# SSD scan: where a group's squares, rounded gates and remainders stand in the queues of ScalarE and VectorE

## The chip, the cores and the metric

The kernel runs on one core of a Trainium2 chip. The metric is the device time of one execution in microseconds (us): 1591.27 before the change, the median of three runs (1589.19 to 1595.38). A core has five engines, each of which works off its own queue of instructions in the written order: TensorE (PE in the profile; PEld is its weight load), VectorE (DVE), ScalarE (ACT), GpSimd (POOL) and SyncE (SP, which issues the transfers). They wait for each other through semaphores only, written out by hand.

## The reference, cut to what matters

One step of a two-layer trunk on 384 tokens (128 of context, 256 latent) with 1024 channels, in float32. The first layer's mixer is a Mamba-2 scan (SSD) in both directions with 32 heads in 8 groups, chunks of 128 tokens:

```python
acum = jnp.cumsum(dtc * a_neg.reshape(ng, nr), axis=2)
decay = jnp.exp(jnp.where(mask, acum[:, :, :, None] - acum[:, :, None, :], -jnp.inf))
scores = jnp.einsum('bcign,bcjgn->bcijg', cc, bc)
y_intra = jnp.einsum('bcijgr,bcjgrp->bcigrp', scores[..., None] * decay, xdt)
states = jnp.einsum('bcqgn,bcqgr,bcqgrp->bcgrpn', bc, decay_end, xdt)
y_inter = jnp.einsum('bcign,bcgrpn,bcigr->bcigrp', cc, s_prev, jnp.exp(acum))
...
y = y_f + flip_seq(y_b) + xs * d_skip[:, None]
y = rms_norm(y.reshape(bsz, seqlen, SSD_D_INNER) * jax.nn.silu(z), norm_w)
return y @ w_out, s_f, s_b
```

The gated rows y * silu(z) go through an RMS norm (so the sum of their squares is needed) and then into the output projection. In the kernel a float32 product with weights is made of three passes over rounded parts: an operand is split into a rounded value ("hi") and its remainder ("lo", the value minus the rounded one).

## The kernel before, in words

The scan takes the groups g = 0 to 7 one after the other, and in each the three chunks u = 3g, 3g+1, 3g+2 (context, first and second latent chunk). All tiles stay in SBUF. Five functions, `ssd_pe`, `ssd_act`, `ssd_dve`, `ssd_pool` and `ssd_sp`, write out the queue of each engine by hand; nothing is planned or reordered. Work for the next group begins before a group is done: the token rows, masked scores and segment sums of chunks 3g+3 to 3g+5 stand in group g's part of the queues.

TensorE, per chunk: `turn_rows` transposes the chunk and forms its scores, `segment(u)` sums the decay exponents of both directions from rounded rows (`decay_rows`, GpSimd) and their remainders (`rows_lo`, ScalarE, L1322), `outputs(u)` (L1500) multiplies the decayed scores. Per group: `states` (L1462), `entry_decays` (L1475) and `entry` (L1487) for the states that enter the two latent chunks. Between these it multiplies blocks of the conditioning weights for the other sub-layers (`conditioning`, L402): 14 blocks in group 0, then 10 a group in groups 1 to 3 and 9 in groups 4 to 7. `conditioning(g, 0, 2)`, right behind `states(g)`, waits until VectorE has added the bias to the block before, `conditioned(g-1)` (L413).

ScalarE: `token_rows` (L1285) copies the transposed rows, `decays` (L1289) takes the exponent of a segment, `entry_decays` (L1301) that of the entry decays. `gates_out(g)` makes, for the two tiles of a finished group, two squares (L1307 or L1311) and two rounded gates `yhi` (L1313).

VectorE: `masked` (L1572) masks the scores, `decayed` (L1580) multiplies them by the decays, `new_state` (L1591) carries the states, `entered` (L1598 to L1601) weights the entering states' rows, `gated_out` (L1609 to L1617) adds them, the skip and the gate. `gates_lo(g)` makes the two remainders `ylo` of a finished group (L1622); it waits for `yhi`.

GpSimd makes `xdt`, `xw`, `sdec` and the rounded decay rows, and at the end of a group's part sums the squares (`square_sums`, L1406). Behind the last group it splits the first two blocks of the output weights (`split_one_lo`, L332).

Behind the scan, VectorE finishes the modulation vectors of all sub-layers in small steps (L1667 to L1672). `back_act` waits for the last of them before ScalarE's third split of output weights (L320), and the output projection (`back_pe`, L819 to L821) takes its tiles of gates in order: tiles 0 to 7 in its first block, 8 to 15 in its second.

Of the kernel before, what the change touches and what calls it, by code (L numbers as in the profile page):

```python
# [122 lines left out]
def trunk(nc, io):  # L123
    ctx = ExitStack()
    with ctx:
# [72 lines left out]
        def v(name):  # L198
            a, b = VEC[name]
            return vec[:, a:b]  # L200
# [121 lines left out]
        def split_first(act, name):  # L322

            for k in range(2):
                split_hi(act, phase[name], Idx(k))
# [198 lines left out]
        def ada_rows(act, bank, n):  # L524
            act.activation(arow[:, :], ps[:, bank, 0:P], ACT.Copy).then_inc(ada_row, 1)
# [719 lines left out]
        def h4(ap):  # L1245
            return ap.rearrange("p (h n) -> p h n", h=4)
# [6 lines left out]
        def ssd_begin(eng):  # L1253
            eng.wait_ge(dt_tok, 2)
            eng.wait_ge(tok_split, 2)
            eng.wait_ge(dt_dec, 1)
            eng.wait_ge(conv_silu, 2 + CONV_T)
            eng.wait_ge(blk_done, phase["ssd_in"].own0 + N_IN + SPL)
# [17 lines left out]
        def ssd_act(act):  # L1276
            ssd_begin(act)

            def token_rows(u):
                g, c = u // 3, u % 3  # L1280
                act.wait_ge(s_a, u + 1)
                if g >= 2:
                    act.wait_ge(s_xdt, u - 5)
                    act.wait_ge(s_st, 2 * g - 2)
                act.activation(xtok[:, g % 2, c, :], ps[:, 0, 0:TOK], ACT.Copy).then_inc(s_xtok, 1)  # L1285

            def decays(u):
                act.wait_ge(s_seg, u + 1)
                act.activation(ps[:, 1 + u % 2, :], ps[:, 1 + u % 2, :], ACT.Exp).then_inc(s_exp, 1)  # L1289

            def state_out(g):
                act.wait_ge(s_st, 2 * g + 1)
                if g:
                    act.wait_ge(s_out[(g - 1) % 2], 16 * ((g - 1) // 2 + 1))
                act.activation(st_sb[:, :], ps[:, 4, :], ACT.Copy).then_inc(s_stout, 1)

            def entry_decays(g, k):
                act.wait_ge(s_eb, 2 * g + k + 1)
                if g:
                    act.wait_ge(s_bw, 2 * g - 1 + k)  # L1300
                act.activation(e_in[:, k].rearrange("p d n -> p (d n)"), ps[:, 4 + k, :], ACT.Exp).then_inc(s_ee, 1)  # L1301

            def gates_out(g):
                act.wait_ge(s_v, 3 * g + 3)
                for t in (2 * g, 2 * g + 1):
                    if g == 0:
                        act.activation(rms_sum[t % 2][:, :], gate[:, t, :], ACT.Square).then_inc(rms_sq, 1)  # L1307
                    else:
                        if g > 1:
                            act.wait_ge(rms_add, t - 3)  # L1310
                        act.activation(rms_new[t % 2][:, :], gate[:, t, :], ACT.Square).then_inc(rms_sq, 1)  # L1311
                for t in (2 * g, 2 * g + 1):
                    act.activation(yhi[:, t, :], gate[:, t, :], ACT.Copy, scale=nw[:, t:t + 1]).then_inc(y_hi, 1)  # L1313

            def rows_lo(u):
                g, c = u // 3, u % 3
                if u:
                    act.wait_ge(s_seg, u)
                for d in range(2):
                    for h in range(4):  # L1320
                        n = 4 * g + 32 * d + h
                        i = act.activation(seg_lo[:, d, h * P:(h + 1) * P], masks[:, 1 + d, :], ACT.Copy,  # L1322
                                           scale=tok_lo[:, c, n:n + 1].bitcast(F32))
                i.then_inc(s_rlo, 1)

            nw = v("ssd_norm")
            rows_lo(0)
            for c in range(NCH):
                token_rows(c)
            decays(0)  # L1330
            rows_lo(1)
            for g in range(SSD_G):
                more = g + 1 < SSD_G
                decays(3 * g + 1)
                state_out(g)
                rows_lo(3 * g + 2)
                act.wait_ge(s_stout, g + 1)
                act.dma_start(io["o_ssd"][g], st_sb[:, :].rearrange("p (d n) -> p d n", d=2)).then_inc(s_out[g % 2], 16)
                entry_decays(g, 0)
                if more:  # L1340
                    token_rows(3 * g + 3)
                decays(3 * g + 2)
                if g:
                    gates_out(g - 1)
                entry_decays(g, 1)
                if more:
                    rows_lo(3 * g + 3)
                    token_rows(3 * g + 4)
                    decays(3 * g + 3)
                    rows_lo(3 * g + 4)  # L1350
                    token_rows(3 * g + 5)
                act.wait_ge(ada_used, ADA_1 + ADA_G[g + 1])
                act.wait_ge(ada_tr, g + DT)
                ada_rows(act, 3, ADA_G[g + 1] - ADA_G[g])
            split_first(act, "ssd_out")
            gates_out(SSD_G - 1)
# [205 lines left out]
        def ssd_dve(dve):  # L1562
# [12 lines left out]
            def decayed(u):  # L1575
                dve.wait_ge(s_exp, u + 1)
                dve.wait_ge(s_gm, u + 1)
                if u >= 2:
                    dve.wait_ge(s_y, u - 1)
                dve.tensor_tensor(ge_s[:, u % 2].rearrange("p d (h n) -> p d h n", h=4),  # L1580
                                  h4(ps[:, 1 + u % 2, :]).unsqueeze(1).to_broadcast([P, 2, 4, P]),
                                  gm_s[:, u % GM].unsqueeze(2).to_broadcast([P, 2, 4, P]), ALU.mult).then_inc(s_ge, 1)

            def new_state(g):
                b = g % 2
                dve.wait_ge(s_st, 2 * g + 2)
                if g >= 2:
                    dve.wait_ge(s_in, 2 * g - 2)
                for d in range(2):
                    dve.wait_ge(s_dec, 2 * g + d + 1)  # L1590
                    dve.tensor_tensor(s1[:, b, d, :], sdec[:, d, :], ps[:, 5, d * 256:(d + 1) * 256],  # L1591
                                      ALU.add).then_inc(s_new, 1)

            def entered(g, k):
                n = 2 * g + k
                f, w = ps[:, 4 + k, 0:256], ps[:, 4 + k, 256:512]
                dve.wait_ge(s_in, n + 1)
                dve.tensor_tensor(w, w, e_in[:, k, 1, :], ALU.mult).then_inc(s_fw, 1)  # L1598
                dve.tensor_tensor(y_in[:, k, :], f, e_in[:, k, 0, :], ALU.mult).then_inc(s_fw, 1)
                dve.wait_ge(s_fw, 2 * n + 2)  # L1600
                dve.tensor_tensor(y_in[:, k, :], y_in[:, k, :], w, ALU.add).then_inc(s_bw, 1)  # L1601
# [17 lines left out]
            def gates_lo(g):  # L1619
                for t in (2 * g, 2 * g + 1):  # L1620
                    dve.wait_ge(y_hi, t + 1)
                    dve.scalar_tensor_tensor(ylo[:, y_lo_tile(t), :], gate[:, t, :], nw[:, t:t + 1],  # L1622
                                             yhi[:, t, :].bitcast(F32), ALU.mult, ALU.subtract).then_inc(y_lo, 1)

            def conditioned(g):
                dve.wait_ge(ada_tr, g + DT + 1)
                ada_bias(dve, 3, ADA_1 + ADA_G[g], ADA_G[g + 1] - ADA_G[g]).then_inc(ada_ready, 1)
# [5 lines left out]
            for g in range(SSD_G):  # L1633
                u = 3 * g
                decayed(u + 1)
                if g:
                    conditioned(g - 1)
                new_state(g)
                gated_out(u)
                masked(u + 3)  # L1640
                decayed(u + 2)
                if g:
                    gates_lo(g - 1)
                entered(g, 0)
                masked(u + 4)
                gated_out(u + 1)
                if g + 1 < SSD_G:
                    decayed(u + 3)
                entered(g, 1)
                masked(u + 5)  # L1650
                gated_out(u + 2)
# [10 lines left out]
            for m in range(1, 2 * DEPTH):  # L1662
                lay, part = m // 2, 3 * (m % 2)
                g, b = (v(x).rearrange("p (n t) -> p n t", n=4)[:, m - 1, :].unsqueeze(2).to_broadcast([P, DT, 2])
                        for x in ("ln_g", "ln_b"))
# [9 lines left out]
        def y_lo_tile(t):  # L1675

            return t // 2 + 8 * (t % 2)
# [1541 lines left out]
```

## Time and profile before

| | |
|---|---|
| median of three runs | 1591.27 us (1589.19 to 1595.38) |
| profiled execution | 1593.25 us, span of its trace 1591.3 us |
| busy: TensorE, VectorE, ScalarE, GpSimd | 97%, 55%, 50%, 57% of the span |
| granted TensorE clock, mean | 0.983 of full speed |
| the SSD scan | from about 238 to 404 us |
| one of the groups 1 to 6 | 19.0 to 19.8 us |

The shares are means over the whole program. Only the stretch of the scan, 10% of the span, holds the instructions that the change moves, so the rows below are cut from it. A busy time is that of an engine's own instructions; the bracket behind a row gives the idle time just before it and what ended it.

### The profile page before, as it was taken

The page shows a single profiled execution, that of the slowest core. Times are in us where ns is not written, and L with a number is a line of the kernel's source. Part 1 is how long each engine was busy: PE and PEld are TensorE (multiplying, and loading weights), DVE is VectorE, ACT ScalarE, POOL GpSimd, SP SyncE. Part 2 cuts the span into 40 slices and gives each one's busy share as a digit, 9 for nine tenths or more (in the row PEclk, how much of TensorE's full clock was granted, in tenths as well). Part 3 has the DMA queues.
Part 4 walks back from the last instruction along what each step waited for, and adds up shares of the span by engine and source line. Part 5 has one row for each costly group of instructions (what it writes and reads, how often), then busy time and mean ns, then how long its engine had stood idle before and what let it go on. Part 6 is the DMA issues. An engine that isn't in the chain of part 4 may idle for free.

```text
span 1591.3 us, 31239 instructions
## 1 busy us (share of the span) xinstructions
PE 1536.7 (97%) x11879; PEld 1460.3 (92%) x11879; DVE 871.2 (55%) x1814; ACT 799.3 (50%) x1461; POOL 905.8 (57%) x516
## 2 busy tenths in 40 slices
PE   8999998999999999999999999999989999999996
PEld 6999996877999999999999989888789999999996
DVE  3453104777437777712673448598883357777323
ACT  3655436776336444423776554555554345544323
POOL 2555556677572555557245556787764725555552
PEclk9999999999999999999999999999989999999998
DMA  9333437877451343434124323101123523434431
GB/s 378 121 120 119 127 125 251 307 285 277 148 165 55 119 132 122 156 112 153 53 93 161 107 89 110 42 28 49 38 87 114 154 80 106 132 120 141 133 122 40
DMA packets 58020, 209.67 MB, mean 132 GB/s; under 512 B 6321, under 2 KB 6449, under 8 KB 57649
## 3 DMA queue, kind: packets, MB, share of 16 engines
q1 hardware_dynamic: 56752, 205.96, 39.3%
q10 hardware_dynamic: 1152, 2.10, 0.4%
q8 instruction: 81, 1.33, 0.3%
q14 instruction: 35, 0.28, 0.1%
HBM read 200.63 MB, written 7.41 MB: 131 GB/s over the span
## 4 chain that ended last, share of the span: by engine, by line
PE 70%; issue 9%; DVE 8%; POOL 7%; ACT 3%; DMA 2%; POOLq 0%; DVEq 0%; SPq 0%; ACTq 0%
PE ps L911 6%; PE ps L913 6%; PE ps L912 6%; PE ps L819 6%; PE ps L821 6%; PE ps L820 6%; POOL wlo L332 4%; PE ps L2905 3%; PE ps L2907 3%; PE ps L2906 3%; PE ps L1155 3%; PE ps L1157 3%; PE ps L1156 3%; PE ps L402 2%; DVE ps L2478 1%
## 5 line engine op out<-in xcount | busy, mean ns | idle before, releaser
L332 POOL TENSOR_TENSOR wlo<-raw,whi 128x1024 fp32r<-128x1024 f32 (+1 forms) x191 | 484.2, 2536 | 412.1 <-ACT whi L320 411.7
L320 ACT ACTIVATE whi<-raw 128x1024 fp32r<-128x1024 f32 (+1 forms) x237 | 261.4, 1103 | 500.0 <-PE ps L821 185.4
L911 PE MATMUL ps<-hhi,whi 128*128 128x384 f32 x656 | 219.8, 335 | 2.5 <-POOL wlo L332 2.0
L985 DVE SCALAR_TENSOR_TENSOR evac<-ps,vec,evac 128x189 f32<-128x189 f32 (+3 forms) x440 | 166.5, 412 | 97.1 <-ACT evac L926 67.5
L913 PE MATMUL ps<-hhi,wlo 128*128 128x384 f32 x656 | 219.2, 334 | 0.0
L912 PE MATMUL ps<-hlo,whi 128*128 128x384 f32 x656 | 219.1, 334 | 0.0
L2670 POOL TENSOR_TENSOR wlo<-raw,whi 128x1024 fp32r<-128x1024 f32 x46 | 111.2, 2418 | 124.2 <-ACT whi L320 124.2
L2905 PE MATMUL ps<-hhi,whi 128*128 128x384 f32 x368 | 126.9, 345 | 0.7 <-POOL wlo L2670 0.7
L911 PEld LDWEIGHTS ps<-hhi,whi 128*128 128x128 f32 x656 | 123.1, 188 | 4.4 <-issue 3.2
L2907 PE MATMUL ps<-hhi,wlo 128*128 128x384 f32 x368 | 123.9, 337 | 0.0
L2906 PE MATMUL ps<-hlo,whi 128*128 128x384 f32 x368 | 123.8, 337 | 0.0
L879 DVE SCALAR_TENSOR_TENSOR xr<-ps,ada,xr 128x128 f32<-128x128 f32 x64 | 23.8, 413 | 182.0 <-PE ps L821 181.8
L912 PEld LDWEIGHTS ps<-hlo,whi 128*128 128x128 f32 x656 | 123.2, 188 | 0.0
L913 PEld LDWEIGHTS ps<-hhi,wlo 128*128 128x128 f32 x656 | 123.1, 188 | 0.0
L1155 PE MATMUL ps<-hhi,whi 128*128 128x384 f32 x360 | 120.5, 335 | 0.6 <-POOL wlo L332 0.6
L1157 PE MATMUL ps<-hhi,wlo 128*128 128x384 f32 x360 | 120.3, 334 | 0.0
L1156 PE MATMUL ps<-hlo,whi 128*128 128x384 f32 x360 | 120.3, 334 | 0.0
L819 PE MATMUL ps<-ghi,whi 128*128 128x384 f32 x352 | 118.6, 337 | 1.3 <-POOL wlo L332 1.3
L821 PE MATMUL ps<-ghi,wlo 128*128 128x384 f32 x352 | 117.6, 334 | 0.0
L820 PE MATMUL ps<-glo,whi 128*128 128x384 f32 x352 | 117.6, 334 | 0.0
L819 PE MATMUL ps<-yhi,whi 128*128 128x384 f32 x256 | 87.1, 340 | 2.3 <-POOL wlo L332 2.3
L820 PE MATMUL ps<-ylo,whi 128*128 128x384 f32 x256 | 85.6, 334 | 0.0
(379 smaller groups left out, 3587.7 us busy)
## 6 DMA issues: line engine op xcount, KB each, us to landing
raw<-w_in_in SPq DMA_DIRECT2D x98, 512.0 KB, 3.5
raw<-w_up_in SPq DMA_DIRECT2D x88, 512.0 KB, 3.5
raw<-w_ada_in SPq DMA_DIRECT2D x80, 512.0 KB, 4.5
raw<-w_down_in SPq DMA_DIRECT2D x32, 704.0 KB, 4.1
raw<-w_out_in SPq DMA_DIRECT2D x32, 512.0 KB, 3.8
first_ada<-w_ada_in SPq DMA_DIRECT2D x16, 512.0 KB, 10.0
qe<-e_keep SPq DMA_DIRECT2D x8, 512.0 KB, 6.8
s<-s_ssd_in SPq DMA_DIRECT2D x8, 256.0 KB, 4.2
```

What stands on the lines that cost most here:

```text
L320: act.activation(whi[:, z.mod(SPL), 0:p.kt * P], raw[:, b.mod(RAW), 0:p.kt * P], ACT.Copy).then_inc(hi_ready, 1)
L332: pool.tensor_tensor(wlo[:, z.mod(SPL), 0:p.kt * P], raw[:, b.mod(RAW), 0:p.kt * P], whi[:, z.mod(SPL), 0:p.kt * P].bitcast(F32), ALU.subt ...
L819: pe.matmul(out, a, rhi[:, h, :], start=(r == 0), stop=False)
L820: pe.matmul(out, a, rlo[:, l, :], start=False, stop=False)
L821: mm = pe.matmul(out, b, rhi[:, h, :], start=False, stop=(r == 2 * p.kt - 1))
L911: pe.matmul(out, a, hhi[:, k, :], start=(k == 0), stop=False)
L912: pe.matmul(out, a, hlo[:, k, :], start=False, stop=False)
L913: mm = pe.matmul(out, b, hhi[:, k, :], start=False, stop=(k == DT - 1))
L1155: pe.matmul(out, a, hhi[:, k, :], start=(k == 0), stop=False)
L2905: pe.matmul(out, a, hhi[:, k, :], start=(k == 0), stop=False)
L2906: pe.matmul(out, a, hlo[:, k, :], start=False, stop=False)
L2907: mm = pe.matmul(out, b, hhi[:, k, :], start=False, stop=(k == DT - 1))
```

## The change

ScalarE: `gates_out(g - 1)` stood between `decays(3 * g + 2)` and `entry_decays(g, 1)`. It now stands behind `token_rows(3 * g + 4)` and ahead of `decays(3 * g + 3)`; what was between comes sooner. VectorE: `gates_lo(g - 1)` stood between `decayed(u + 2)` and `entered(g, 0)`. It now stands between `decayed(u + 3)` and `entered(g, 1)`. In the last group, where there is no `decayed(u + 3)`, it follows `gated_out(u + 1)`. No instruction is added, removed or altered, and no wait is.

```diff
                     token_rows(3 * g + 3)
                 decays(3 * g + 2)
+                entry_decays(g, 1)
+                if more:
+                    rows_lo(3 * g + 3)
+                    token_rows(3 * g + 4)
                 if g:
                     gates_out(g - 1)
-                entry_decays(g, 1)
-                if more:
-                    rows_lo(3 * g + 3)
-                    token_rows(3 * g + 4)
+                if more:
                     decays(3 * g + 3)
                     rows_lo(3 * g + 4)
                     token_rows(3 * g + 5)
...
                 masked(u + 3)
                 decayed(u + 2)
-                if g:
-                    gates_lo(g - 1)
                 entered(g, 0)
                 masked(u + 4)
                 gated_out(u + 1)
                 if g + 1 < SSD_G:
                     decayed(u + 3)
+                if g:
+                    gates_lo(g - 1)
                 entered(g, 1)
                 masked(u + 5)
                 gated_out(u + 2)
```

## Rows read from the trace of the kernel before

**Rows 1.** The page's first part: busy us, share of span, instructions.
```profile
PE 1536.7 (97%) x11879; PEld 1460.3 (92%) x11879; DVE 871.2 (55%) x1814; ACT 799.3 (50%) x1461; POOL 905.8 (57%) x516
```

**Rows 2.** Busy time of one scan group: PE, PEld, DVE, ACT, POOL; clock, DMA.
```profile
329.50:348.50 19.00, 18.87 (x280) 15.47 (x279) 14.22 (x29) 13.76 (x39) 14.55 (x15) 1.00 0.84 302
```

**Rows 3.** List of waits, 240 to 405: us in total, times, longest.
```profile
PEld ps L402 <- DVE ada L413: 4.1, 7, 0.8
```

**Rows 4.** Timeline of VectorE at a group's end: start, us, instruction, idle before.
```profile
324.60 1.22 DVE L1580 TENSOR_TENSOR ge_s<-ps,gm_s 128x1024 f32<-128x1024 f32 x1 [0.19 <-ACT ps L1289]
...
327.32 0.42 DVE L1572 TENSOR_TENSOR gm_s<-ps,masks 128x256 f32<-128x256 f32 x1 [0.38 <-ACT xtok L1285]
...
329.20 1.23 DVE L1580 TENSOR_TENSOR ge_s<-ps,gm_s 128x1024 f32<-128x1024 f32 x1
330.34 0.17 DVE L413 TENSOR_TENSOR ada<-ps,vec 128x20 f32<-128x20 f32 x1
```

**Rows 5.** Timeline of TensorE, conditioning blocks that waited.
```profile
321.16 0.65 PE L402 MATMUL ps<-raw,scond 128*32 128x128 f32 x16 [0.52 <-DMA raw<-w_ada_in]
...
330.56 0.81 PEld L402 LDWEIGHTS ps<-raw,scond 128*32 128x32 f32 x32 [0.47 <-DVE ada L413]
```

**Rows 6.** Timeline of all engines, group 3: entry decays, squares, rounded gates, next decays.
```profile
316.32 1.09 PE L1475 MATMUL ps<-masks,small 128*64 128x128 f32 x16
...
316.92 0.93 ACT L1311 ACTIVATE rms_new<-proj 128x384 f32<-128x384 f32 x2
...
317.75 1.11 ACT L1313 ACTIVATE yhi<-proj,vec 128x384 fp32r<-128x384 f32 x2
...
323.99 0.58 ACT L1289 ACTIVATE ps<-ps 128x512 f32<-128x512 f32 x1 [1.94 <-PE ps L1452]
```

**Rows 7.** Remainders and GpSimd: line L1622 (ns min/median/max), then timelines of groups 1 and 3.
```profile
L1622 DVE SCALAR_TENSOR_TENSOR ylo<-proj,vec,yhi x16: 618/967/1961, 280.2 to 407.1; 128x384 fp32r<-128x384 f32 x16
...
280.18 1.50 POOL L1377 TENSOR_TENSOR xw<-xtok,small 128x256 f32<-128x256 f32 x2
280.24 1.85 DVE L1622 SCALAR_TENSOR_TENSOR ylo<-proj,vec,yhi 128x384 fp32r<-128x384 f32 x2
...
317.92 1.90 POOL L1366 TENSOR_TENSOR seg_hi<-masks,tok_hi 128x1024 fp32r<-128x1024 f32 x1
318.39 2.73 DVE L1622 SCALAR_TENSOR_TENSOR ylo<-proj,vec,yhi 128x384 fp32r<-128x384 f32 x2
...
327.37 0.61 POOL L1377 TENSOR_TENSOR xw<-xtok,small 128x256 f32<-128x256 f32 x1 [4.63 <-ACT xtok L1285]
```

**Rows 8.** Timeline of all engines at the end of group 5.
```profile
362.03 0.58 ACT L1289 ACTIVATE ps<-ps 128x512 f32<-128x512 f32 x1 [1.22 <-PE ps L1452]
...
362.81 1.22 DVE L1580 TENSOR_TENSOR ge_s<-ps,gm_s 128x1024 f32<-128x1024 f32 x1
...
365.37 0.42 DVE L1572 TENSOR_TENSOR gm_s<-ps,masks 128x256 f32<-128x256 f32 x1 [0.23 <-ACT xtok L1285]
```

**Rows 9.** Timeline of the scan's end and the output projection's start.
```profile
401.06 4.72 POOL L332 TENSOR_TENSOR wlo<-raw,whi 128x1024 fp32r<-128x1024 f32 x2 [3.88 <-ACT whi L320]
...
401.87 0.43 DVE L1598 TENSOR_TENSOR ps<-ps,e_in 128x256 f32<-128x256 f32 x1
...
411.30 2.00 ACT L320 ACTIVATE whi<-raw 128x1024 fp32r<-128x1024 f32 x2 [4.60 <-DVE vec L1672]
...
414.84 0.45 PE L819 MATMUL ps<-yhi,whi 128*128 128x384 f32 x1 [0.22 <-POOL wlo L332]
```

**Rows 10.** Busy time and granted clock (behind POOL's) around two TensorE gaps.
```profile
250.00:252.00 2.00, 0.91 (x3) 0.77 (x4) 0.00 (x0) 0.95 (x4) 1.14 (x2) 0.92 1.01 414
252.00:254.00 2.00, 2.00 (x6) 1.61 (x5) 0.72 (x1) 0.58 (x1) 1.28 (x1) 0.50 0.82 336
...
1016.00:1018.90 2.90, 0.78 (x70) 0.67 (x63) 2.85 (x5) 2.81 (x7) 2.90 (x4) 1.00 0.13 48
1018.90:1022.00 3.10, 3.10 (x63) 2.43 (x63) 3.07 (x4) 1.72 (x4) 3.10 (x4) 0.63 0.03 8
```

More of the change, by code:

```diff
@@ L1342, in ssd_act @@
                 decays(3 * g + 2)
-                if g:
-                    gates_out(g - 1)
                 entry_decays(g, 1)
@@ L1348, in ssd_act @@
                     token_rows(3 * g + 4)
+                if g:
+                    gates_out(g - 1)
+                if more:
                     decays(3 * g + 3)
@@ L1641, in ssd_dve @@
                 decayed(u + 2)
-                if g:
-                    gates_lo(g - 1)
                 entered(g, 0)
@@ L1648, in ssd_dve @@
                     decayed(u + 3)
+                if g:
+                    gates_lo(g - 1)
                 entered(g, 1)
```

## The prediction

> **What bounds the kernel now.** I read the page first: TensorE is busy for 97% of the span [rows 1], so a change off TensorE counts only where TensorE waits for it. Then the busy time by stretch: one scan group (19 us) has TensorE busy 18.87 us, VectorE 14.22, ScalarE 13.76, GpSimd 14.55 [rows 2]. No other engine is full, and TensorE has hardly any idle time to give back: the reader is to see that the change can gain little and can lose much. The list of waits then says which wait is left: the first conditioning block of a group (L402) waits for VectorE's bias add L413, 7 times, 4.1 us on the weight side [rows 3]. About 0.2 us of each is a gap that other blocks have as well. That wait ends VectorE's chain at the end of a group, which is next in the timeline: `decayed(u+3)` at 324.60, `entered(g,1)`, `masked(u+5)` at 327.32 after 0.38 us idle (for ScalarE's token rows), `gated_out(u+2)`, `decayed(u+4)` at 329.20, L413 at 330.34 [rows 4]; TensorE starts L402 at 330.56 [rows 5]. So from `decayed(u+3)` on, VectorE already sets the end of every group, with 0.38 us of slack.
>
> **ScalarE's part.** Nothing is added; two squares and two rounded gates move from behind `decays(3g+2)` to behind `token_rows(3g+4)`. They take 316.92 to 318.86, 1.94 us [rows 6]. In their new place they stand ahead of `decays(3g+3)`, where ScalarE waits 1.94 us for TensorE's segment today (start 323.99) [rows 6]. What moves ahead is not quite free: `entry_decays(g,1)` must now wait for L1475, which starts at 316.32 and runs 1.09 us, so it begins at 317.41 instead of the squares at 316.92: 0.49 us lost. The queue is through at 323.99 - 1.94 + 0.49 = 322.54, 1.4 us ahead of the segment. I cost ScalarE's move at nothing; the idle 1.94 us is its cover, and if it were gone the score decays, and with them the chain on VectorE, would be late by the excess, at most 1.94 us a group. The segment on TensorE needs `rows_lo(3g+3)`, which comes sooner; no TensorE wait in today's list was for it after group 0, so nothing is gained. GpSimd's sums of squares stand behind `state_decay`, around 328, after the new place of the squares: nothing.
>
> **VectorE's part.** The two remainders (L1622) leave the place ahead of `entered(g,0)` and go between `decayed(u+3)` and `entered(g,1)`: into the chain that ends in L413. Behind them stand `entered`, `masked`, `gated_out`, `decayed(u+4)`, L413, and TensorE's whole queue waits for that. What their old place gives back is idle time: `decayed(u+3)` waits for ScalarE's exponent, not for them, except that in groups 4 to 6 VectorE is a little late. In group 5 the exponent ends at 362.03 + 0.58 = 362.61 and `decayed` starts at 362.81 [rows 8]: 0.16 us comes back beside the usual 0.04.
>
> What do two remainders cost in the new place? Today a pair takes 1.85 us in groups 1 and 2, 2.73 in group 3 [rows 7], because GpSimd is at work. The rows show how: two GpSimd products of 0.61 us each take 1.50 instead of 1.22 while the pair runs, and the pair ends at 280.24 + 1.85 = 282.09, 0.41 us after the GpSimd pair at 281.68. A product of 1.90 us at 317.92 stretches the pair to 2.73. The two engines take turns: each remainder waits out a whole GpSimd instruction, then runs some 0.4 us. In the new place, 325.7 to 326.7, GpSimd is idle: it waits 4.63 us for the token rows and starts at 327.37 [rows 7]. Bounds for the pair are 2 x 0.41 = 0.82 and 1.85; the shortest one alone took 0.618 from start to end [rows 7], and VectorE's instructions overlap by about 0.1. I take 0.95, near the lower end, for GpSimd's idle stretch covers it. The chain absorbs 0.38 us of it in groups 1 to 3 and 0.23 + 0.16 = 0.39 in group 5 (groups 4 and 6 alike). So 0.95 - 0.39 = 0.56 us for each of the six boundaries (groups 1 to 6; group 0 has no remainders, and behind group 7 no conditioning follows): 6 x 0.56 = 3.4 us. It is lost on TensorE in full, as L402 waits already.
>
> **The last group.** There `decayed(u+3)` is absent, so group 6's remainders come directly behind `gated_out(22)`, at 401.87, where `entered(7,1)` starts today [rows 9]. At that time GpSimd splits the first two output weights: 4.72 us for two from 401.06, 2.36 each, the first to 403.42. By the turns of [rows 7] remainder one runs 403.42 to 403.89, split two 403.89 to 406.25, remainder two to about 406.65. `entered(7,1)` starts 4.7 us late, and with it the last gated output, group 7's gates, and the small modulation steps of VectorE; ScalarE's third output split (411.30, waiting for the last of these) and TensorE's third output block (414.84, already waiting 0.22 us for that split) come 4.7 us later [rows 9]. Split two is late by 0.5 us, still ahead of TensorE's second block. No remainder runs beside a weight split in the trace, so both ends stand: without exclusion the shift is the pair alone, 0.95 us; with it 4.7. I take 4.7, since every pair of rows shows turns.
>
> The Trainium skill, page "SBUF — State Buffer", section "Who interferes with whom", says that a VectorE instruction with two SBUF inputs and a GpSimd instruction that reads SBUF cannot run together, and that the one issued second blocks fully. By it the last group costs the 4.7 us above; had remainders and splits run together, 0.95. Rows 7 agree for GpSimd's products; for the weight split no row decides.
>
> **Given back and added.** TensorE's wait for a weight transfer in group 3, 0.52 us [rows 5], goes when the group starts later with its transfers under way: -0.5 (0 to -1). And the clock: where TensorE idled, the granted clock fell to 0.50 of full speed, the 1.2 GHz level: in 250 to 252 it was busy 0.91 us of 2.00, and in 252 to 254 the clock was 0.50; near 1017 it was busy 0.78 of 2.90, then 0.63 over 3.10 us [rows 10]. Lost time: 0.08 x 2 + 0.50 x 2 = 1.16 and 0.37 x 3.1 = 1.15 us. In the last group TensorE now stands still for some 1.6 us ahead of its second block's last tiles (they need group 7's remainders) and about 3.1 ahead of the third block, longer than these gaps: +1.2, between 0 and 2.4. The 0.5 us stalls of the boundaries are too short to compare with them: 0.
>
> Sum: 3.4 + 4.7 - 0.5 + 1.2 = 8.8 us. The profiled execution took 1593.25 us (span 1591.3 and 1.95 around it), so 1602.1 for such a one; it lay 1.98 us above the median 1591.27, hence **1600.1 us**. A measurement tells 0.5% (8.0 us) from no change; the forecast is just past that.
>
> **The rivals.** (a) The turns are not as strict for weight splits, and the tail costs 0.95 with no clock loss: 3.4 + 0.95 - 0.5 = 3.9, 1595.1 us. For: no row shows this pair of operations. Against: three GpSimd forms took turns with L1622. (b) The pair costs in its new place what it costs today, 1.85 us, because GpSimd's products come earlier than I reckon, or ScalarE's four operations do not fit: 6 x (1.85 - 0.39) = 8.8, with 4.7 - 0.5 + 1.2: 14.2, 1605.5 us. Against it: GpSimd's 4.63 us idle. (c) The other side: the remainders hide altogether and TensorE's wait for L413 goes, since entered and masked rows of the group's first half come over a microsecond sooner. That gains the 4.1 us less 7 x 0.2, so -2.7: 1588.6 us. It decides where a pair costs under 0.39 us, the chain's slack; the shortest single remainder is 0.618. (d) As forecast, but the clock holds: 1598.9 us.
>
> **How the numbers follow.** Forecast with clock loss 0.42, (d) 0.15, (a) 0.20, (b) 0.13, (c) 0.06, and 0.04 for what I have not seen. With some 2 us of scatter (the runs shown spread from 1589.19 to 1595.38), slower by over 0.5%, above 1599.2: 0.27 + 0.07 + 0.13 + 0.02 = 0.49. Faster by over 0.5%: no case reaches it by itself; 0.05 with the unseen. The rest, 0.46, within 0.5%. The range reaches to (a) and most of the way to (b): 1594.5 to 1604.5.
>
> **What would show it.** Right: the remainders at the end of a group take about 0.95 us a pair; L413 and TensorE's L402 start about 0.8 us apart from TensorE's last state product instead of 0.3; groups 1 to 6 are 0.5 us longer; ScalarE still waits for the segment ahead of its decays; in the last group remainder one ends with the first weight split, remainder two with the second, and TensorE idles about 3 us ahead of its third output block, with a clock below 1.00 behind it. Wrong: groups of unchanged length, or remainders running inside a weight split. A loop loss of over 1 us a group would say that the pair or ScalarE's queue was mis-sized.

## The result and the profile after

The changed kernel takes 1602.37 us, median of five runs (1600.26 to 1603.74), against 1591.2 us (1589.19 to 1595.38, five runs): ratio 1.006 with a 95% interval of 1.0044 to 1.0075, that is 7.0 to 11.9 us slower. The profiled execution took 1601.72 us, its span 1599.8.

The first part of the page. TensorE's busy time is 1.3 us below that of [rows 1], so on balance the 8.5 us of longer span are idle time; what a slower clock adds at one place has to be offset at another (below):

```profile
PE 1535.4 (96%) x11879; PEld 1460.2 (91%) x11879; DVE 867.0 (54%) x1814; ACT 800.6 (50%) x1461; POOL 902.3 (56%) x516
```

The list of waits between 240 and 440 us (us in total, times, longest). The wait for the bias has grown from 4.1 to 7.3 us on the weight side [rows 3], and the output projection now waits 1.4 us for remainders and 2.9 us for a weight split:

```profile
PEld ps L402 <- DVE ada L413: 7.3, 7, 1.4
PE ps L402 <- DVE ada L413: 4.4, 6, 1.0
PE ps L819 <- POOL wlo L332: 3.6, 2, 2.9
PE ps L819 <- DVE ylo L1623: 1.4, 1, 1.4
```

The timeline at the end of group 3 (lines of VectorE have moved by one; compare [rows 4 to 6]):

```profile
322.48 1.11 ACT L1313 ACTIVATE yhi<-proj,vec 128x384 fp32r<-128x384 f32 x2
...
324.26 0.58 ACT L1289 ACTIVATE ps<-ps 128x512 f32<-128x512 f32 x1 [0.67 <-PE ps L1453]
...
324.88 1.23 DVE L1581 TENSOR_TENSOR ge_s<-ps,gm_s 128x1024 f32<-128x1024 f32 x1 [0.20 <-ACT ps L1289]
...
326.02 1.14 DVE L1623 SCALAR_TENSOR_TENSOR ylo<-proj,vec,yhi 128x384 fp32r<-128x384 f32 x2
...
327.07 0.43 DVE L1599 TENSOR_TENSOR ps<-ps,e_in 128x256 f32<-128x256 f32 x1
...
327.64 0.62 POOL L1378 TENSOR_TENSOR xw<-xtok,small 128x256 f32<-128x256 f32 x1 [5.20 <-ACT xtok L1285]
...
328.20 0.42 DVE L1573 TENSOR_TENSOR gm_s<-ps,masks 128x256 f32<-128x256 f32 x1
...
331.11 0.17 DVE L413 TENSOR_TENSOR ada<-ps,vec 128x20 f32<-128x20 f32 x1
...
331.33 1.08 PE L402 MATMUL ps<-raw,scond 128*32 128x128 f32 x32 [0.55 <-DVE ada L413]
```

The reader is to see the chain of [rows 4] with the remainders in it: they occupy VectorE from 326.02 to 327.07, 1.05 us, while GpSimd stands idle (it starts at 327.64 after 5.20 us); the idle 0.38 us ahead of L1573 has gone; and from `decayed(u+3)` to the bias it is 331.11 - 324.88 = 6.23 us instead of 330.34 - 324.60 = 5.74. (1.05 less 0.38 would be 0.67 us; the other 0.18 were smaller gaps between the chain's instructions, which went as well.) ScalarE still waits 0.67 us for the segment ahead of its decays, so its moved work fits. From one L402 to the next, groups 4 and 5 take 19.56 us each (18.97 and 18.98 before). From group 1's first L402 (271.92) to group 7's (390.43) it is 118.51 us, against 115.00 (272.62 to 387.62): 3.5 us.

The end of the scan, as [rows 9]:

```profile
403.80 5.04 POOL L332 TENSOR_TENSOR wlo<-raw,whi 128x1024 fp32r<-128x1024 f32 x2 [3.21 <-ACT whi L320]
...
404.61 4.64 DVE L1623 SCALAR_TENSOR_TENSOR ylo<-proj,vec,yhi 128x384 fp32r<-128x384 f32 x2
...
415.17 0.41 PE L819 MATMUL ps<-yhi,whi 128*128 128x384 f32 x1 [1.41 <-DVE ylo L1623]
...
418.41 2.00 ACT L320 ACTIVATE whi<-raw 128x1024 fp32r<-128x1024 f32 x2 [4.41 <-DVE vec L1673]
...
421.94 0.69 PE L819 MATMUL ps<-yhi,whi 128*128 128x384 f32 x1 [2.95 <-POOL wlo L332]
```

The pair of remainders starts 0.8 us after the first weight split and ends at 409.25, 0.41 us behind the second one (408.84). From group 7's first L402 to the third output block it is 31.51 us instead of 27.22: 4.3 us. The stretches around that gap (length, busy PE, PEld, DVE, ACT, POOL, then the granted clock), to be read beside [rows 10]:

```profile
419.00:421.94 2.94, 0.00 (x1) 0.01 (x1) 0.16 (x1) 2.91 (x4) 2.40 (x2) 0.78 0.00 0
421.94:424.00 2.06, 2.06 (x6) 2.06 (x7) 1.59 (x4) 0.34 (x1) 2.06 (x1) 0.50 0.33 103
424.00:426.00 2.00, 2.00 (x8) 2.00 (x8) 0.17 (x1) 0.00 (x0) 0.23 (x1) 0.50 0.69 207
426.00:428.00 2.00, 2.00 (x9) 2.00 (x8) 0.00 (x0) 0.00 (x0) 0.00 (x0) 0.62 0.52 211
```

The third block runs at 0.50, the 1.2 GHz level, for most of its length. From its start to the start of the fifth block's split on GpSimd TensorE does the same 33 products without a pause, first before, then after:

```profile
414.84:420.53 5.69, 5.69 (x33) 5.69 (x34) 1.81 (x5) 1.47 (x3) 2.30 (x2) 1.00 0.65 184
```

```profile
421.94:430.17 8.23, 8.23 (x33) 8.23 (x34) 1.76 (x4) 1.47 (x3) 2.29 (x2) 0.66 0.38 127
```

That is 8.23 us instead of 5.69: the clock costs 2.5 us.

So 3.5 + 4.3 + 2.5 = 10.3 us are lost in these two places. The medians differ by 11.2 us, the two profiled spans by 8.5 only, and the rest of the span accounts for the difference. The changed execution reached group 1 0.7 us earlier (271.92 against 272.62). In the second layer, which the change does not touch, TensorE's clock dipped in the execution of before and not in the same stretch of after; from the product at 829.34 (L2936; 838.96 in after) to the one at 840.66 (L2913; 847.15) it is 11.32 us before and 8.19 after, 3.1 less. First before, then after:

```profile
782.00:840.00 58.00, 56.33 (x320) 54.87 (x319) 37.97 (x76) 42.12 (x68) 24.61 (x11) 0.94 0.27 82
```

```profile
791.60:849.60 58.00, 56.34 (x338) 55.15 (x337) 38.52 (x78) 44.33 (x72) 25.70 (x12) 1.00 0.27 82
```

Further on it is the other way round. Both executions wait there for ScalarE, 1.87 us each, but only in after is the clock at half a little later, which costs 1.6 us (from these products to the L1890 ones, 17.14 us before and 18.71 after). Another 0.5 us comes in smaller pieces up to the end. Before, a wait and the stretch behind it, then the same after:

```profile
948.90 0.66 PE L1885 MATMUL ps<-masks,ge 128*128 128x128 f32 x4 [1.87 <-ACT ge L2127]
```

```profile
949.00:952.40 3.40, 3.40 (x22) 3.40 (x23) 3.11 (x4) 2.57 (x3) 2.58 (x2) 1.00 0.31 124
```

```profile
955.39 0.66 PE L1886 MATMUL ps<-masks,ge 128*128 128x128 f32 x4 [1.87 <-ACT ge L2128]
```

```profile
956.60:960.00 3.40, 3.40 (x12) 3.40 (x12) 3.36 (x6) 1.48 (x2) 2.14 (x1) 0.50 0.06 19
```

In all: -0.7 + 10.3 - 3.1 + 1.6 + 0.5 = 8.6, which is the 8.5 up to rounding.

### The profile page after: what moved, and what is told of

Its sections match the earlier page's. It is cut to its first block, busy times and chain, and to the rows that moved or that the text cites. A ratio compares the mean times of both kernels' runs of the same rounds, so it can differ in the third digit from the quotient of the medians.

```text
span 1599.8 us, 31239 instructions
## 1 busy us (share of the span) xinstructions
PE 1535.4 (96%) x11879; PEld 1460.2 (91%) x11879; DVE 867.0 (54%) x1814; ACT 800.6 (50%) x1461; POOL 902.3 (56%) x516
## 4 chain that ended last, share of the span: by engine, by line
PE 69%; DVE 10%; issue 9%; POOL 7%; ACT 3%; DMA 2%; SPq 0%; POOLq 0%; DVEq 0%; ACTq 0%
PE ps L911 6%; PE ps L913 6%; PE ps L912 6%; PE ps L819 6%; PE ps L820 6%; PE ps L821 6%; POOL wlo L332 4%; PE ps L2906 3%; PE ps L2908 3%; PE ps L2907 3%; PE ps L1155 3%; PE ps L1156 3%; PE ps L1157 3%; PE ps L402 2%; DVE ps L2479 1%
```

## The experiments

Each ratio is that of a run to runs of the kernel before on the same chip; the rows come from one profiled execution of each kernel.

**Loop only.** The last group's remainders go back to their old place; groups 1 to 6 stay changed.

```diff
                 decayed(u + 2)
+                if g + 1 == SSD_G:
+                    gates_lo(g - 1)
                 entered(g, 0)
...
-                if g:
+                if g and g + 1 < SSD_G:
                     gates_lo(g - 1)
                 entered(g, 1)
```

> The changed kernel, but in the last group the remainders stand where they stood before (ahead of the first entered state); groups 1 to 6 stay as changed. Theory (two separate losses: 3.5 us at the group ends, and 4.3 us plus a clock loss of 2.5 us behind the last group, both from the remainders beside the weight splits): only the loop's loss is left, 3.5 us over before, ratio about 1.002; TensorE's third output block waits 0.2 us again and the clock behind it is 1.00. Rival (the loss behind the scan comes from the later end of the loop, for instance from transfers that fall elsewhere): the wait of about 3 us and the half clock stay, ratio 1.006.

Ratio 1.0024 (1.001 to 1.0039). The group ends are those of the changed kernel, and TensorE waits 0.25 us ahead of the third output block, which runs at full clock (its start to the fifth split: 5.67 us):

```profile
349.83 1.08 PE L402 MATMUL ps<-raw,scond 128*32 128x128 f32 x32 [0.88 <-DVE ada L413]
...
416.89 0.45 PE L819 MATMUL ps<-yhi,whi 128*128 128x384 f32 x1 [0.25 <-POOL wlo L332]
```

The loss behind the scan thus comes from the last group's two instructions, not from the later end of the loop.

**Last group only.** The kernel before, with only the last group's remainders moved.

```diff
-                if g:
+                if g and g + 1 < SSD_G:
                     gates_lo(g - 1)
                 entered(g, 0)
...
                     decayed(u + 3)
+                if g + 1 == SSD_G:
+                    gates_lo(g - 1)
                 entered(g, 1)
```

> The kernel before, with the remainders moved in the last group alone. Theory: groups 1 to 6 as before; the pair of remainders takes about 4.6 us beside the weight splits, TensorE waits about 1.4 and 3 us in the output projection, and its clock falls to half behind that: 4.3 + 2.5 = 6.8 us over before, ratio 1.0043. Rival (the two losses are one, and the tail alone costs only the pair, 1 us): ratio 1.0006.

Ratio 1.0043 (1.0027 to 1.0059). Two instructions moved past others cost 4 to 9 us:

```profile
401.11 5.05 POOL L332 TENSOR_TENSOR wlo<-raw,whi 128x1024 fp32r<-128x1024 f32 x2 [4.46 <-ACT whi L320]
401.91 4.66 DVE L1622 SCALAR_TENSOR_TENSOR ylo<-proj,vec,yhi 128x384 fp32r<-128x384 f32 x2
...
419.25 0.69 PE L819 MATMUL ps<-yhi,whi 128*128 128x384 f32 x1 [2.94 <-POOL wlo L332]
```

```profile
420.00:422.00 2.00, 2.00 (x8) 2.00 (x8) 1.45 (x4) 0.00 (x0) 1.53 (x1) 0.50 0.81 248
```

The loop's 1.0024 and this 1.0043 add up to 1.0067, beside 1.006 for the whole.

**Bias first**, in the changed kernel.

```diff
-                decayed(u + 1)
                 if g:
                     conditioned(g - 1)
+                decayed(u + 1)
```

> The changed kernel with the conditioning bias of a group ahead of the decayed scores of its second chunk instead of behind them. Theory (the loop's loss reaches TensorE only through its wait for the bias): that wait goes, and with it 7 times 0.75 to 1.25 us, so the groups 1 to 6 last some 18.7 to 19.1 us, less than before; the tail's 6.8 us stay: about 4.5 us over before, ratio 1.003. Rival (the remainders delay TensorE through the decayed scores or the states as well): another wait appears in the same place, and the groups stay at 19.6 to 20.0 us, ratio 1.006.

Ratio 1.0036 (1.0023 to 1.005). The list of waits from 262 to 395 shows the 7.3 us gone to 1.0, and TensorE's own row for L413 is no longer in it; from one bias to the next, a group lasts 18.83 us instead of 19.56 (350.67 to 370.23 in the changed kernel):

```profile
PEld ps L402 <- DVE ada L413: 1.0, 3, 0.3
```

```profile
347.05 0.17 DVE L413 TENSOR_TENSOR ada<-ps,vec 128x18 f32<-128x18 f32 x1
365.88 0.17 DVE L413 TENSOR_TENSOR ada<-ps,vec 128x18 f32<-128x18 f32 x1
```

The loop's loss reaches TensorE through its wait for the bias and nothing else: with that wait gone, the groups are shorter than before the change (18.97), though the remainders still stand in the chain. The kernel before with the same edit (below) comes to the same 18.83 us.

**One SBUF input.** The last pair of moved remainders takes its second input from PSUM, so its two tiles hold other values than the remainders.

```diff
-                                             yhi[:, t, :].bitcast(F32), ALU.mult, ALU.subtract)
+                                             ps[:, 2, 0:TOK] if g == SSD_G - 2 else yhi[:, t, :].bitcast(F32),
+                                             ALU.mult, ALU.subtract)
```

> The changed kernel, but the last moved pair of remainders (group 6) takes its second input from PSUM instead of SBUF, so these two tiles get other values than the remainders. Same instruction, same place, same length. Theory (a VectorE instruction with two SBUF inputs and a GpSimd weight split exclude each other): the pair takes about 1.1 us instead of 4.64, starts while the first split runs, the split pair takes 4.7 instead of 5.04, and the tail costs 1.1 us with no clock loss: 3.5 + 1.1 = 4.6 us over before, ratio 1.003. Rival (the pair waits for something else, such as the rounded gates, or VectorE is slow there): it takes 4 to 5 us again, ratio 1.006.

Ratio 1.0036 (1.0021 to 1.0051). The pair takes 1.13 us and runs wholly inside the first weight split, which is not lengthened:

```profile
403.58 4.72 POOL L332 TENSOR_TENSOR wlo<-raw,whi 128x1024 fp32r<-128x1024 f32 x2 [3.18 <-ACT whi L320]
...
404.36 1.13 DVE L1623 SCALAR_TENSOR_TENSOR ylo<-proj,vec,ps 128x384 fp32r<-128x384 f32 x2
...
418.20 0.44 PE L819 MATMUL ps<-yhi,whi 128*128 128x384 f32 x1 [1.07 <-POOL wlo L332]
```

```profile
420.00:422.00 2.00, 2.00 (x14) 2.00 (x13) 0.44 (x1) 0.00 (x0) 0.51 (x1) 1.00 0.62 231
```

Only the place of one input differs from the changed kernel, and 3.5 us of VectorE time go with it. The rivals fall: the wait for the rounded gates is still there, and VectorE does the same work. Nor are two SBUF inputs slow by themselves: in groups 1 to 6 of the changed kernel, where GpSimd stands idle, the pair takes 1.14 us with them. In the output projection the wait of 1.41 us is gone and that of 2.95 us is 1.07, and the clock stays at 1.00.

**Bias first, in the kernel before** (the same edit).

> The kernel before, with the conditioning bias of a group ahead of the decayed scores of its second chunk. Theory (TensorE's wait for the bias is the last one in groups 1 to 6): TensorE's seven waits for the bias go and the groups last about 18.8 us (as with the bias first in the changed kernel) instead of 19.0 to 19.1; a gain of 7 times 0.28 to 0.43 us less what transfers take back, 1 to 2.5 us, ratio 0.9990. Rival (some other engine holds the groups at 19.0 us): unchanged, ratio 1.000; at this size the times will hardly tell, the rows will.

Ratio 1.0002 (0.9989 to 1.0015). The groups are shorter: from group 1's bias to group 7's 385.20 - 271.44 = 113.76 us, before 115.01. But in the last group TensorE now waits for weights:

```profile
397.15 0.65 PE L402 MATMUL ps<-raw,scond 128*32 128x128 f32 x16 [2.70 <-DMA raw<-w_ada_in]
```

The gain in the loop is given back there, and more of it by the clock than by the wait. From group 7's first L402 to the first output block it is 404.58 - 386.22 = 18.36 us, before 403.48 - 387.62 = 15.86. TensorE's waits in that stretch come to 2.94 us (2.14 before), 0.8 more; and the clock behind the long one falls, by the measure of [rows 10] 0.42 x 4.05 = 1.7 us:

```profile
397.15:401.20 4.05, 4.04 (x44) 3.21 (x46) 1.18 (x3) 0.34 (x2) 0.00 (x0) 0.58 0.81 282
```

The times don't tell the kernels apart.

**VectorE's part alone**: the second hunk of the change without the first.

```diff
                 decayed(u + 2)
-                if g:
-                    gates_lo(g - 1)
                 entered(g, 0)
...
                 if g + 1 < SSD_G:
                     decayed(u + 3)
+                if g:
+                    gates_lo(g - 1)
                 entered(g, 1)
```

> VectorE's part of the change alone: the remainders move, ScalarE's squares and rounded gates stay where they were. Theory (ScalarE's part costs and gains nothing): as the changed kernel, six group ends with a longer wait for the bias, pair of 4.6 us in the last group, ratio 1.006. Rival (ScalarE's part pays for some of the loss, or causes some): clearly different from 1.006, below 1.003 or above 1.009.

Ratio 1.006 (1.0044 to 1.0076), the whole loss:

```profile
369.67 1.08 PE L402 MATMUL ps<-raw,scond 128*32 128x128 f32 x32 [0.88 <-DVE ada L413]
...
403.79 4.67 DVE L1622 SCALAR_TENSOR_TENSOR ylo<-proj,vec,yhi 128x384 fp32r<-128x384 f32 x2
```

**ScalarE's part alone**: the first hunk without the second.

```diff
+                entry_decays(g, 1)
+                if more:
+                    rows_lo(3 * g + 3)
+                    token_rows(3 * g + 4)
                 if g:
                     gates_out(g - 1)
-                entry_decays(g, 1)
-                if more:
-                    rows_lo(3 * g + 3)
-                    token_rows(3 * g + 4)
+                if more:
                     decays(3 * g + 3)
```

> ScalarE's part of the change alone: squares and rounded gates move behind the second token rows, the remainders stay ahead of the first entered states. Theory: VectorE must wait for the rounded gates at the old place of the remainders, about 4 to 5 us a group, so entered states, masked scores, gated output and decayed scores behind come about 2.5 us late, and TensorE waits about 2 us a group: 6 x 2 = 12 us over before, last group small, ratio 1.007 to 1.010; the two parts only go together. Rival (ScalarE's new order is what gives time back, and VectorE has the slack): ratio at or below 1.002.

Ratio 1.0064 (1.0046 to 1.0082), smaller than I wrote, though the interval reaches into the range. VectorE waits for the rounded gates, and TensorE for the masked scores behind them:

```profile
PE ps L1442 <- DVE gm_s L1573: 10.2, 7, 1.9
```

```profile
326.29 1.15 DVE L1623 SCALAR_TENSOR_TENSOR ylo<-proj,vec,yhi 128x384 fp32r<-128x384 f32 x2 [3.86 <-ACT yhi L1313]
```

The longest of these waits, 1.9 us, is in group 0 and is there in all kernels; the six others are 1.1 to 1.6 us where I had reckoned 2. The mechanism held, the size was over. Alone, ScalarE's part hurts; in the changed kernel it neither costs nor gains anything that the ratios of 1.006 with and without it show.

**Gap filled.** Four products into an unread bank behind the total of the squares, in the changed kernel.

```diff
                 if n == 0 and j == 1:
                     rms_total(pe)
+                    for _ in range(4):
+                        pe.matmul(ps[:, 4, 0:TOK], ones, rms_sum[0][:, :], start=True, stop=True)
```

> The changed kernel with four matrix products into a bank that nobody reads, behind the total of the squares: 2.9 us of TensorE work in the gap of 2.95 us ahead of the third output block. Theory (2.5 us of the loss is the half clock behind that gap): the third block starts as late as in the changed kernel but runs at clock 1.00 and takes 4.2 us instead of 6.7, ratio 1.006 - 0.0016 = 1.0045. Rival (the third block is slow for another reason, weights or transfers): the block still takes 6 to 7 us, ratio 1.006.

Ratio 1.005 (1.0033 to 1.0066), too near 1.006 for the times to decide; the rows do. The third block starts at 423.42, as late behind group 7's first L402 as in the changed kernel (31.62 us against 31.51), and is followed by the fifth split at 429.09, 5.67 us, as before the change (L826 is the four products, eight instructions):

```profile
420.32 2.83 PE L826 MATMUL ps<-rms_sum,masks 128*128 128x384 f32 x8
...
423.42 0.44 PE L819 MATMUL ps<-yhi,whi 128*128 128x384 f32 x1 [0.28 <-POOL wlo L332]
```

```profile
424.00:426.00 2.00, 2.00 (x14) 2.00 (x13) 1.62 (x4) 0.00 (x0) 1.72 (x1) 1.00 0.70 199
```

So the slow third block was the clock's doing, and it is TensorE's idle time ahead of it that let the clock fall.

**Both losses undone**: the changed kernel with the bias first and the last group's remainders at the old place (the edits of the first and third experiment together).

> The changed kernel with both losses undone: the bias first, and the last group's remainders at their old place. Theory (these two account for the whole loss): TensorE's waits for the bias and the waits of 1.4 and 3 us in the output projection go, the clock behind the scan is 1.00; what the groups gain is taken back by the weight transfers of the last group, as with the bias first in the kernel before; ratio 0.999 to 1.001. Rival (a third loss is left): ratio 1.002 or more.

Ratio 0.9998 (0.9989 to 1.0007): no third loss that the times show. What the groups gain is taken back, in the loop by waits for transfers (0.53 us in group 3, 0.65 in group 6) and in the last group. There the waits are no longer than before the change (2.02 us against 2.14), but the clock falls behind the one below and costs 0.46 x 3.71 = 1.7 us, by the measure of [rows 10]:

```profile
397.49 1.01 PE L402 MATMUL ps<-raw,scond 128*32 128x128 f32 x16 [1.69 <-DMA raw<-w_ada_in]
```

```profile
397.49:401.20 3.71, 3.71 (x40) 2.94 (x40) 1.61 (x3) 0.00 (x0) 0.53 (x1) 0.54 0.87 298
```

**Bias first, blocks moved**: the kernel before with the bias first and three conditioning blocks taken from the last group.

```diff
-        ADA_G = (0, 14, 24, 34, 44, 53, 62, 71, ADA_2)
+        ADA_G = (0, 14, 24, 34, 44, 54, 64, 74, ADA_2)
```

> The kernel before with the bias first, and the conditioning blocks dealt out as 14, 10, 10, 10, 10, 10, 10, 6 instead of 14, 10, 10, 10, 9, 9, 9, 9 a group, so that the last group has three transfers fewer to wait for. Theory (with the bias first, the gain of 1 to 2 us is taken back by TensorE's wait for transfers in the last group, 2.70 us): that wait shrinks below 1 us, the scan ends 2 to 3 us sooner than in the kernel before, ratio 0.9983. Rival (transfers bound the scan as a whole): the wait moves into groups 4 to 6, ratio 1.000.

Ratio 0.9988 (0.9977 to 0.9999), 1591.27 us beside 1592.94: about 2 us faster than before, if barely clear of no change. TensorE's longest wait for transfers in the last group is 0.29 us instead of 2.70; one of 0.64 us comes in group 6, so part of the rival is there too. The first output block starts at 401.54 (403.48 before), but part of the gain is lost again where ScalarE's third split waits 4.42 us for the small modulation steps and TensorE 1.71 us for that split. The clock holds behind this gap:

```profile
401.54 0.44 PE L819 MATMUL ps<-yhi,whi 128*128 128x384 f32 x1 [0.41 <-POOL wlo L332]
...
414.36 0.44 PE L819 MATMUL ps<-yhi,whi 128*128 128x384 f32 x1 [1.71 <-POOL wlo L332]
```

```profile
414.36:420.03 5.67, 5.67 (x33) 5.67 (x34) 1.76 (x4) 1.48 (x3) 2.31 (x2) 1.00 0.63 185
```

## Why the prediction was right, and where it was off

The time lay in the range (1602.37 us, forecast 1600.1, range 1594.5 to 1604.5), slower by 0.6%, and each of the two mechanisms is shown by an experiment of its own.

- **ScalarE's move at nothing**: right. VectorE's part alone has the same ratio, and ScalarE still waits 0.66 to 0.91 us for the segment in groups 1 to 6 of the profile after. For group 3 I had 1.4 us and it is 0.67: the entry decays cost 0.45 us as laid out (0.49), but the segment itself comes 0.7 us sooner behind the group's first L402 (12.50 us against 13.22).
- **The group ends**: right. The pair was put at 0.95 us and takes 1.05; the loss at 0.56 us a group, and it is 0.59 in groups 4 and 5. That it runs through L413 is shown by the bias first.
- **Transfers, -0.5**: not found in the profiled execution. The wait of 0.52 us in group 3 went [rows 5], and that group is 0.22 us shorter than before in place of 0.59 longer; but other waits came, such as 0.30 us in group 2 and 0.27 on the weight side in group 6, so over groups 1 to 6 the loss is 3.5 us, which is 6 x 0.59 with nothing given back. The term is not settled: in the profiles of loop only, one SBUF input, VectorE's part alone and gap filled, which have VectorE's new order in groups 1 to 6, these took 117.87 to 118.10 us instead of 118.51, and in the last group only, with the loop of before, 114.53 instead of 115.00.
- **The last group**: 4.7 us forecast, 4.3 measured, 4.6 with the last group alone (419.25 - 387.42 against 27.22). That it comes from GpSimd and VectorE excluding each other over two SBUF inputs is shown by the one SBUF input. Rival (a) had the pair run beside the split; it falls. Remainder two ended 0.41 us behind the second split (laid out: 0.40).
- **The clock, 1.2 us**: the sign was right, and the size half of what the profiled execution shows. I took it from dips behind shorter gaps [rows 10]; here it cost 2.5 us, and in the three other executions with the same gap 1.5 (last group only), 2.8 (bias first) and 1.3 (VectorE's part alone), by the same difference of starts against 5.69. So 1.2 lies just under the shorter of these dips. What sets the length was not tried.

Sum: forecast 8.8, found 10.3 in the two places; most of the difference is the clock and the transfers. Rival (b), a pair as dear as beside GpSimd, fell by the 1.05 us. Rival (c), the hidden pair, fell with the chain's idle time. Rival (d), a clock that holds behind the third block's gap, happened only where the gap was filled or short.

## What to carry to other kernels

An instruction moved off a busy stretch of its engine is not free where it lands: look for the chain that ends in the bounding engine's wait, and place it where the engine is idle ahead of that chain, not inside. Then look at what GpSimd does at the new place: one microsecond of VectorE work with two SBUF inputs took 4.6 because GpSimd was in the middle of two long operations. And count the clock behind a gap of TensorE, which here was a quarter of the loss, but count it as a range: the same gap cost 1.3 to 2.8 us in four executions.

## What the runs showed of the hardware

The same VectorE instruction takes 1.13 us a pair beside GpSimd's weight split with one of its two tensors in PSUM, 4.64 us with both in SBUF, and 1.14 us with both in SBUF where GpSimd stands idle. The Trainium skill, page "SBUF — State Buffer", section "Who interferes with whom", says that VectorE with at most one SBUF input, outside its two-port modes, does not contend with GpSimd, and with two inputs against a GpSimd read does; both halves agree with the first two of these numbers.

The granted clock fell to 0.50 behind TensorE gaps of 1.4 and 2.95 us close together, in all four profiled kernels that have both. It stayed at 1.00 in the one SBUF input, where one gap of 1.07 us is left, and in the gap filled, where the first gap is there (1.39 us) and the second is filled down to 0.28. The length of a gap does not decide alone: behind one of 1.69 us (both losses undone) the clock was 0.54 over 3.71 us, behind one of 1.71 us (blocks moved) it stayed at 1.00, and behind the gap of 1.87 us in the second layer it was 0.50 in the execution of after and 1.00 in that of before.
